# The low halves of the output weights on GpSimd in place of VectorE, in a hybrid decoder layer with a mixture of experts

## The reference, cut to what matters

```
xn  = rmsnorm(x)
mix = sigmoid(ga) * (branch_a @ proj_a) + sigmoid(gb) * (branch_b @ proj_b) + sigmoid(gc) * (branch_c @ proj_c)
x   = x + mix @ w_out                      # w_out is 1024 x 1024
x   = x + hier_moe(rmsnorm(x))             # 64 experts, two per token
y   = rmsnorm(x)
```

## Time and profile before

| what | us |
|---|---|
| median of three runs (1857.49 to 1858.94) | 1857.85 |
| the profiled execution | 1858.85 |
| its span, first to last instruction | 1857.1 |
| busy: PE / PEld / DVE / ACT / POOL | 1739.9 / 1485.3 / 582.4 / 445.4 / 248.6 |

### The profile page before, as it was taken

How to read it: one execution, slowest core, us unless ns; L and a number is a source line. 1 busy time by engine, 2 the same in 40 slices (tenths; PEclk the granted TensorE clock), 3 DMA queues, 4 the chain that set the end, 5 groups by cost and what they waited for, 6 DMA issues and landing times.

```text
span 1857.1 us, 27357 instructions
## 1 busy us (share of the span) xinstructions
PE 1739.9 (94%) x11384; PEld 1485.3 (80%) x11384; DVE 582.4 (31%) x1045; ACT 445.4 (24%) x790; POOL 248.6 (13%) x312
## 2 busy tenths in 40 slices
PE   8999999999999999999999999997989888888877
PEld 8999999999999989999999998886545444444442
DVE  5000102442223232265124338665222211111115
ACT  6222224632232222321222015211111111111113
POOL 0003210001111111000000000001222222222220
PEclk9999999999999999999999999998999999999998
DMA  4222224245445554557445353215999999999997
GB/s 157 95 94 95 71 81 131 95 137 159 127 142 183 161 162 149 169 191 256 151 180 178 94 183 107 80 68 227 377 419 419 420 420 419 418 418 419 420 386 294
DMA packets 159478, 406.31 MB, mean 219 GB/s; under 512 B 20342, under 2 KB 102134, under 8 KB 134779
## 3 DMA queue, kind: packets, MB, share of 16 engines
q1 hardware_dynamic: 137402, 344.22, 50.1%
q0 software_dynamic: 21952, 60.34, 8.5%
HBM read 340.62 MB, written 79.60 MB: 226 GB/s over the span
## 4 chain that ended last, share of the span: by engine, by line
PE 86%; issue 5%; DMA 3%; DVE 3%; ACT 1%; DVEq 1%; SPq 1%; ACTq 0%; POOLq 0%
PE ps L1957 16%; PE ps L1959 16%; PE ps L1958 16%; PE ps L2260 12%; PE ps L2156 8%; PE ps L2282 6%; PE ps L2247 2%; PE ps L2261 2%; PE ps L2271 1%; DMA FY<-ytok 1%; PE ps L1970 1%; PE ps L2054 1%; PE ps L2194 1%; PE ps L2045 1%; DMA SG<-feat 1%
## 5 line engine op out<-in xcount | busy, mean ns | idle before, releaser
L1957 PE MATMUL ps<-XH,WH 128*128 128x384 f32 (+1 forms) x1152 | 384.4, 334 | 0.2 <-DVE QK L1454 0.2
L1959 PE MATMUL ps<-XH,WL 128*128 128x384 f32 (+1 forms) x1152 | 376.9, 327 | 0.0
L1958 PE MATMUL ps<-XL,WH 128*128 128x384 f32 (+1 forms) x1152 | 376.8, 327 | 0.0
L2260 PE MATMUL ps<-E,XT 128*64 128x256 f32 x1024 | 246.7, 397 | 77.6 <-issue 76.7
L2260 PEld LDWEIGHTS ps<-E,XT 128*64 128x64 f32 x1024 | 140.8, 142 | 134.6 <-issue 84.5
L2261 PE MATMUL ps<-E,XT 128*64 128x256 f32 x1024 | 248.1, 398 | 0.0
L1957 PEld LDWEIGHTS ps<-XH,WH 128*128 128x128 f32 x1152 | 216.2, 188 | 10.1 <-issue 7.4
L1958 PEld LDWEIGHTS ps<-XL,WH 128*128 128x128 f32 x1152 | 216.4, 188 | 0.5
L1959 PEld LDWEIGHTS ps<-XH,WL 128*128 128x128 f32 x1152 | 216.2, 188 | 0.0
L1957 PE MATMUL ps<-WH,XH 128*128 128x256 f32 (+2 forms) x648 | 184.6, 285 | 4.8 <-DVE XL L1404 4.8
L1410 DVE TENSOR_TENSOR WL<-RAW,WH 128x2048 fp32r<-128x2048 f32 (+1 forms) x34 | 78.1, 2297 | 349.5 <-ACT WH L1131 349.4
(11 more groups left out here) (333 smaller groups left out, 2342.9 us busy)
## 6 DMA issues: line engine op xcount, KB each, us to landing
E<-in_exp_w_dram SPq DMA_DIRECT2D x192, 1024.0 KB, 21.6
RAW<-in_w_in_dram SPq DMA_DIRECT2D x29, 1024.0 KB, 7.8
feat<-OF POOLq DMA_DIRECT2D x20, 1088.0 KB, 8.0
SG<-feat SPq DMA_DIRECT2D x24, 544.0 KB, 4.5
tokd<-OT POOLq DMA_DIRECT2D x10, 1024.0 KB, 7.3
cbuf<-feat SPq DMA_DIRECT2D x16, 544.0 KB, 5.7
X<-in_x_prompt_dram SPq DMA_DIRECT2D x16, 512.0 KB, 3.7
VR<-tokd SPq DMA_DIRECT2D x32, 256.0 KB, 3.1
```

The source lines that it names most:

```text
L1957: pe.matmul(out, hi, mhi, start=start, stop=False)
L1958: pe.matmul(out, hi, mlo, start=False, stop=False)
L1959: return pe.matmul(out, lo, mhi, start=False, stop=stop)
L2260: pe.matmul(ps[0:BR, 2 + b, 0:DE], XT[b][:, turned(k), :], E1[s][:, 1, k, :], start=(k == 0), stop=(k == KD - 1))
```

## The change

The four subtractions move, with their waits and their semaphore, from VectorE's loop to GpSimd's stream, between the zeroing at L1009 and the wait for the mix. The tiles, the order by quarter and the waits of `out_mm` stay as they are.

```diff
             pool.memset(lgt[:, NFULL, :], 0.0)
+
+            def wo_low(i):
+                k = slice(2 * i, 2 * i + 2)
+                pool.wait_ge(wo_hi, i + 1)
+                pool.tensor_tensor(WOl[:, k, :], WOr[:, k, :], WOh[:, k, :].bitcast(F32), ALU.subtract).then_inc(wo_lo, 1)
+            for i in range(4):
+                wo_low(i)
             pool.wait_ge(mix_ready, KD)
...
-            def wo_low(i):
-                k = slice(2 * i, 2 * i + 2)
-                dve.wait_ge(wo_hi, i + 1)
-                dve.tensor_tensor(WOl[:, k, :], WOr[:, k, :], WOh[:, k, :].bitcast(F32), ALU.subtract).then_inc(wo_lo, 1)
...
                 if u in (17, 19):
                     p_low(14 + (u - 17) // 2)
-                if 17 <= u < 21:
-                    wo_low(u - 17)
             mix_low(KD - 1)
```

## The result

| kernel | median, us | lowest to highest of 6 runs | profiled execution | its span | granted clock |
|---|---|---|---|---|---|
| before | 1857.88 | 1856.93 to 1858.94 | 1858.85 | 1857.1 | 0.984 |
| after | 1865.03 | 1864.35 to 1865.68 | 1864.35 | 1862.6 | 0.977 |

The changed kernel takes 7.15 us more; the ratio is 1.0037, with a 95% interval of 1.0026 to 1.0048.

A forecast was written before the change was run, and what follows sets the result against it. VectorE was taken as late in this stage (6.2 or 7.4 us per unit against TensorE's 6.1). Full turns made units 21, 22 and 23 late by 3.4, 4.3 and finally 6.8 us: 1857.85 + 6.8 = 1864.7 us, range 1854.5 to 1867.0.

The forecast's parts named there:

- no effect: First rival: GpSimd's subtractions do not stretch VectorE's operations beside them; -2.8 us, chance 0.22.
- The ceiling: Clean removal of four VectorE subtractions (8.8 us) lets TensorE start unit 22 earlier; worth at most 2.8 us.
- Turns, at the upper bound: VectorE's two-SBUF-operand operations and GpSimd's subtractions never overlap; the later waits the other's whole length; +6.8 us, chance 0.45.
- GpSimd first at the drain: After gate 18's sum, GpSimd's waiting second subtraction goes ahead of VectorE's mix low half, running 1126.0 to 1130.6 us.
- The second rival: Turns, but VectorE goes first when its next operation is only a drain away; +0.8 us, chance 0.28 together with sharing.
- The length of a turn: Each whole GpSimd subtraction takes 4.60 us, as its product over the same 128 x 2048 elements does.
- the third rival: TensorE's 4.8 us standstill ahead of unit 21 lowers its clock; one unit at that level adds another 6; chance 0.05.
- The sign in the trace: VectorE's timeline shows gaps of about 3.3 and 4.6 us ahead of sum and mix low half, ending with GpSimd's subtractions.
- Sharing by fractions: A contested operation takes twice its length; ends near +0.8 us; chance 0.28 together with turns where VectorE goes first.
- A slower copy because of the float32r output: Fourth rival: GpSimd's subtractions take much longer with float32r output; `out_mm` feels it only at 8 us each; no chance given.

The follow-up runs named there:

- e2: Changed kernel with each GpSimd subtraction replaced by two fills of the same tile, which read nothing; 1854.23 us, 0.9980 of before.
- e3b: Changed kernel with each GpSimd subtraction replaced by one copy of the raw weights, reading one tile; 1855.41 us, 0.9987 of before.
- e1: Changed kernel with each GpSimd subtraction cut in four along its columns, 16 pieces in all; 1855.61 us, 0.9986 of before.
- e8: Before, subtractions on VectorE, with two output-weight loads issued behind gate 17's load and two behind chunk 14 and gate 19's; 1852.58 us, ratio 0.9974.
- e9: Loads ordered as in e8, but subtractions on GpSimd in 16 pieces; 1852.52 us, 0.9976 of before.
- e4: Before, subtractions on VectorE, with gate 17's load issued ahead of the four output-weight loads; 1858.26 us, ratio 1.0001.
- e10: Loads ordered as in e8, but whole subtractions on GpSimd; 1861.00 us, 1.0017 of before.

## Why the prediction held

The forecast was 1864.7 us, +6.8; measured are 1865.03 and +7.15. Its mechanism is what happened. That the size came out so close is luck: two errors nearly cancel. The stated range, 1854.5 to 1867.0, takes in the time of no effect as well, so the median alone would decide little between the rivals; the records decide. Times below are against unit 19's start, which was 1.02 us earlier in the execution of after (1115.19, not 1116.21).

| step | forecast, us late | after |
|---|---|---|
| unit 20 | 1.4 early, no wait | no wait |
| unit 21 | 3.4 | 2.8 |
| unit 22 | 4.3 | 3.5 |
| unit 23 | 6.8 | 5.5 |
| first matmul of `out_mm` | 6.8 | 7.1 |

- **The ceiling.** -2.8 us was worked out for a clean removal. e2, with nothing blocked, gives -3.5 by the stage and -3.55 by the medians: right within 0.8. Of the 0.7 that the stage has more, 0.4 are the length of a unit: 6.1 was read from two units that began only as their gate let them, while in e2 the five units from 19 on take 30.1 us (1115.70 to 1145.81), 6.0 each. The other 0.3 lie ahead of unit 19.
- **Turns, at the upper bound.** Right: records of 4.28, 5.51, 4.18 and 5.54 us where 1.29 is the work. Blocked are 19.51 - 4 x 1.29 = 14.35 us, less the 8.8 removed: 5.55, and unit 23 begins 5.5 late. The trace alone had left this open; the Trainium skill (SBUF — State Buffer, Who interferes with whom) had it: a VectorE instruction with two SBUF inputs against a GpSimd one that reads SBUF. The runs agree with three parts of that: whole instructions block (4.28 for 1.29), a GpSimd instruction that only writes does not (1.29 beside a fill), and one SBUF input on VectorE does not (0.94 and 0.47 inside the subtractions; the Trainium skill says so of operations outside VectorE's 2-port modes). The prediction's own reason for the upper bound, that GpSimd is bound by its reads the earlier trace rows, is not what decides: e3b's copy reads one tile, takes hardly longer than a fill (1.90 and 1.81 us), and collides all the same.
- **GpSimd first at the drain.** The second rival was to be decided there. In after the sum ends at 1124.68 with the second subtraction waiting since 1123.49, and the mix low half is issued at 1124.77: GpSimd goes first, as the working had it.
- **The length of a turn was too large.** 4.60 us, taken from GpSimd's product, measured 4.3 to 4.5. The first two turns make 0.4 of the 0.6 us by which unit 21 came earlier than forecast; unit 23 is 1.3 us earlier.
- **The clock was too small.** It was the third rival, at 0.05, with a whole unit at the lower level (+6). It did happen, twice, for about 3.4 us each; one was hidden and one cost unit 23 1.5 us. So the sum of the forecast lacked this term, and its other terms were too large by nearly as much.
- **The sign in the trace was misjudged.** Gaps ahead of the sum and the mix low half were announced. There are none: the blocked time lies inside the records. The ends agree with the turns all the same, and the products did start inside the subtractions.
- **The other rivals.** No effect is refuted by the records. Sharing by fractions is refuted by e1, and in the form forecast, twice the length, by after itself: 1.29 us of work took 4.2 to 5.5. A slower copy because of the float32r output is excluded: 4.3 to 4.5 us against 4.60 with a float32 output.

**Open.** e8 and e9 gain 5.2 and 5.3 us where the stage shows 4.0 and 4.7; the rest may lie in the profiled executions, which are single ones (e8's is the slowest of its runs, e9's the fastest). Which of the waits put the clock down, and what would have kept it up, was not tried. Whether the order of VectorE's operations could be chosen so that only products meet a subtraction was not tried either.

## What to carry to other kernels

Before work goes from VectorE to an idle GpSimd, count the operations of VectorE beside it that read two SBUF tiles: each can be held for one whole GpSimd instruction, so, where VectorE is the engine that is late, the price is those turns less the work removed (here 14.35 - 8.8 us) and what the clock adds (here 1.5). If the work has to move, cut it into pieces about as long as VectorE's own operations (the one size tried here): the same subtractions in 16 pieces were 2.2 us faster than before, in 4 they were 7.15 slower. And look first at what makes the relieved engine late: moving the four loads of `w_out` behind the loads that were needed first, two and two, won 5.2 us with every subtraction left where it was.

## What the runs showed of the hardware

- Blocked time counts as busy. The page of after has VectorE busy for 587.7 us, where before has 582.4, although 8.8 us of work left it. An operation whose longest record is far over its median (1.29 against 5.54 us here) is a sign of it.
- The turns alternate one for one. In e1 every sum, mix low half and weight low half issued from 1121 to 1150 us is 0.9 to 1.1 us longer than by itself, and the median piece is 2338 ns where the shortest is 1279.
- The lower clock came after standstills of 4.16 and 1.96 us of TensorE in after (0.51 and 0.50 in the windows above), while the three waits of 1.2 us each in before left the clock at 1.00. It came after one of 3.62 us in e4 as well. The length of the one wait does not tell: in e10 a wait of 2.65 us left the clock at 1.00 and one of 1.96 us did not.
